# A causal mask added on VectorE in PSUM in place of a matmul with the identity, in a two-layer transformer block

## What is computed

```python
def masked_softmax(s, mask):
    sf = jnp.where(mask, s.astype(jnp.float32), NEG)
    m = jnp.max(sf, axis=-1, keepdims=True)
    e = jnp.where(mask, jnp.exp(sf - m), 0.0)
    p = e / jnp.maximum(jnp.sum(e, axis=-1, keepdims=True), TINY)
    return p.astype(s.dtype)
...
    def blk(args):                                   # latent attention (MLA)
        qb, tq = args
        s = jnp.einsum('bhqd,bhkd->bhqk', qb, k) * scale
        p = masked_softmax(s, tq[:, None] >= pos[None, :])
        return jnp.einsum('bhqk,bhkd->bhqd', p, v)
```

## Time and profile before

| | |
|---|---|
| median of 3 runs | 1611.4 us (1610.57 to 1613.26) |
| the profiled execution: its own time | 1606.89 us |
| the profiled execution: its span | 1605.1 us |
| granted TensorE clock, mean of the core | 0.993 of full speed |
| attention stage of layer 1 | about 152 to 372 us of the span |
| attention stage of layer 2 | about 948 to 1168 us of the span |

### The profile page before, as it was taken

One profiled execution on the slowest core, in us unless ns is written; L12 is line 12 of the kernel. 1 busy time (PEld: TensorE's weight loads), 2 busy tenths in 40 slices (PEclk: granted clock), 3 DMA queues, 4 the chain that ended last, 5 costly groups with the idle time before them and its releaser, 6 DMA issues.

```text
span 1605.1 us, 23249 instructions
## 1 busy us (share of the span) xinstructions
PE 1535.0 (96%) x7566; PEld 1264.9 (79%) x7566; DVE 883.3 (55%) x1342; ACT 722.9 (45%) x1315; POOL 431.5 (27%) x454
## 2 busy tenths in 40 slices
PE   6999999899999999999999999998989999999996
PEld 4888788777788888888888878877867888888885
DVE  5764655665654453535566655556556545444455
ACT  5853666764332222213366546767624322222232
POOL 0301566666111010102011025757750201010010
PEclk9999999999999999999999999999999999999998
DMA  5243221024323232232323412111243222323222
GB/s 186 85 140 125 73 72 66 36 67 145 123 89 103 92 104 92 93 103 92 99 77 128 163 61 65 68 66 41 89 161 105 87 98 92 105 91 100 96 92 105
DMA packets 43526, 155.55 MB, mean 97 GB/s; under 512 B 5312, under 2 KB 5312, under 8 KB 43424
## 3 DMA queue, kind: packets, MB, share of 16 engines
q1 hardware_dynamic: 37440, 134.23, 25.2%
q0 software_dynamic: 5408, 17.95, 3.2%
q10 hardware_dynamic: 576, 2.10, 0.4%
HBM read 143.78 MB, written 10.49 MB: 96 GB/s over the span
## 4 chain that ended last, share of the span: by engine, by line
PE 78%; DVE 8%; issue 6%; ACT 5%; POOL 2%; DMA 1%; DVEq 0%; ACTq 0%; POOLq 0%
PE G L1321 13%; PE G L1323 12%; PE G L1322 12%; PE O L1321 8%; PE O L1322 8%; PE O L1323 8%; PE O L1587 2%; PE T L1563 2%; PE S L1546 2%; POOL wsplit L463 1%; ACT wsplit L562 1%; DVE nmx L1096 1%; PE T L1321 1%; PE T L1322 1%; PE T L1323 1%
## 5 line engine op out<-in xcount | busy, mean ns | idle before, releaser
L562 ACT ACTIVATE wsplit<-stage 128x1024 fp32r<-128x1024 f32 x230 | 243.5, 1059 | 608.7 <-PE G L1323 288.2
L884 DVE TENSOR_TENSOR wsplit<-stage,wsplit 128x1024 fp32r<-128x1024 f32 x190 | 275.6, 1451 | 79.2 <-ACT wsplit L562 79.2
L1321 PE MATMUL G<-xg,wsplit 128*128 128x512 f32 x592 | 244.5, 413 | 15.6 <-DVE xg L888 13.7
L555 POOL TENSOR_TENSOR F<-Y 128x512 f32<-128x512 f32 x64 | 68.4, 1069 | 625.7 <-DVE Y L1291 625.7
L1323 PE MATMUL G<-xg,wsplit 128*128 128x512 f32 x592 | 232.8, 393 | 0.0
L1322 PE MATMUL G<-xg,wsplit 128*128 128x512 f32 x592 | 232.2, 392 | 0.0
L1096 DVE TENSOR_REDUCE nmx<-S 128x1 f32<-128x512 f32 x192 | 93.3, 486 | 106.5 <-PE S L1554 105.1
L719 ACT ACTIVATE F<-S,nmx 128x512 f32<-128x512 f32 x192 | 101.5, 528 | 95.9 <-DVE nmx L1096 95.6
L1321 PEld LDWEIGHTS G<-xg,wsplit 128*128 128x128 f32 x592 | 113.0, 191 | 38.7 <-DVE xg L888 16.2
L1323 PEld LDWEIGHTS G<-xg,wsplit 128*128 128x128 f32 x592 | 111.9, 189 | 24.6
L1321 PE MATMUL G<-area,wsplit 128*128 128x512 f32 x320 | 124.9, 390 | 5.0 <-DVE wsplit L884 5.0
(11 more groups left out here) (249 smaller groups left out, 3086.6 us busy)
## 6 DMA issues: line engine op xcount, KB each, us to landing
stage<-units SPq DMA_DIRECT2D x230, 512.0 KB, 3.3
stage_n<-units_n SPq DMA_DIRECT2D x22, 512.0 KB, 3.5
gates<-Y POOLq DMA_DIRECT2D x32, 256.0 KB, 3.0
E<-gates POOLq DMA_DIRECT2D x16, 256.0 KB, 3.1
F<-gates POOLq DMA_DIRECT2D x16, 256.0 KB, 3.0
x<-x_in ACTq DMA_DIRECT2D x4, 512.0 KB, 11.6
out<-F SPq DMA_DIRECT2D x6, 256.0 KB, 2.1
rope<-tables POOLq DMA_DIRECT2D x1, 768.0 KB, 10.2
```

The costliest lines, as they stand in the source:

```text
L555: pool.tensor_tensor(F[:, m % 2, :], Y[:, m % 2, :], Y[:, m % 2, :], ALU.mult)\
L562: act.activation(wslot(u)[:, 0, :], staged(u), ACT.Copy).then_inc(s_whin if u in SN else s_whi, 1)
L884: dve.tensor_tensor(wslot(u)[:, 1, :], staged(u), wslot(u)[:, 0, :], ALU.subtract)\
L1321: pe.matmul(dst, a(0), b(0), start=first, stop=False)
```

## The change

The identity matmul leaves `scores`, and the last score matmul now closes the group and posts `s_scores`. VectorE, after its wait for `s_scores`, adds the bf16 mask to the last 128 columns of the scores, in place in PSUM, waits for that instruction by a semaphore of its own (`chain`, `s_dvec`), and takes the maximum.

```diff
                 def max_of(i):
                     w = (JOBS[i][3] + 1) * P
                     dve.wait_ge(s_scores, l * NJ + (i + 1))
+                    diagonal = SB[i % 2][:, w - P:w]
+                    chain.mark(dve.tensor_tensor(diagonal, diagonal, causal, ALU.add))
+                    chain.wait()
                     dve.tensor_reduce(nmx[:, i % 4:i % 4 + 1], SB[i % 2][:, 0:w], AX.X, ALU.max, negate=True)\
                         .then_inc(s_max, 1)
...
                     if i < NSA_NJ:
                         for c in range(2):
-                            pe.matmul(dst[:, 0:w], QS[:, 2 * t + e, qt * P:w], KN[:, br, t // 2, c, 0:w],
-                                      start=(c == 0), stop=False)
+                            ins = pe.matmul(dst[:, 0:w], QS[:, 2 * t + e, qt * P:w], KN[:, br, t // 2, c, 0:w],
+                                            start=(c == 0), stop=(c == 1))
                     else:
...
-                        three(dst[:, 0:w], lambda c: MQ[:, t % 2, e, c, qt * P:w], lambda c: MK[:, t % 2, e, c, 0:w],
-                              True, False)
-                    pe.matmul(dst[:, qt * P:w], identb, causal, start=False, stop=True).then_inc(s_scores, 1)
+                        ins = three(dst[:, 0:w], lambda c: MQ[:, t % 2, e, c, qt * P:w],
+                                    lambda c: MK[:, t % 2, e, c, 0:w], True, True)
+                    ins.then_inc(s_scores, 1)
```

## The result

The changed kernel is slower: 1627.3 us median (1626.0 to 1628.1), against 1611.0 us for the kernel before on the same chip; the ratio is 1.0107, with a 95% interval of 1.0086 to 1.0128. I had forecast 1603 us. The two profiled executions have spans of 1626.3 and 1605.1 us.

What follows compares the result with a forecast made beforehand. TensorE was taken to bound most of the attention stages. Terms -24 + 3.5 + 6.4 + 4.2 + 1.6 = -8.3 us gave 1598.6 from the profiled 1606.9, shifted to 1603 us at the median; range 1593 to 1614.

Steps and rivals of the forecast that it cites:

- What bounds the kernel now: Attention stages: TensorE bounds most of the stage, so work removed from it shortens the kernel; another chain ends last in some stretches.
- The mask's time on TensorE: Each of 192 mask matmuls costs TensorE 0.04 + 0.08 us, taken as 0.125 us: 24 us removed.
- Rival 4: TensorE step behind a score group: the 0.08 us stays, only 6.6 us come back; +5.6 us, 1617; chance 0.06.
- Forfeited gain: 3.5 us: At 28 places where TensorE already waits for L1106, removing the mask gains nothing further: 28 x 0.125 us lost.
- The price of a pair: VectorE's add before the maximum: 0.27 us plus 0.03 us dependent wait, 0.30 us each, 58 us of VectorE.
- Rival 3: VectorE between scores and maximum: the add is dear, 0.5 to 0.65 us a pair; +1.7 to +9 us; chance 0.12.
- The slow place of L1076: A small VectorE operation took 0.65 us at one place, 0.18 at another; used as the add's worst price.
- The waits: 6.4 + 4.2 + 1.6 = 12.2 us: New TensorE waits: 28 for L1106 at 0.23 us, 14 score groups at 0.3, 8 value matmuls at 0.2.
- The 104 late maxima: Of 192 VectorE maxima, 104 come late with scores ready; said to carry delays on if the gain is eaten.
- rival 2: Room at TensorE's waits shrinks further, twice as many score groups become tight at 0.5 us: +1.5 us, 1613; chance 0.15.
- the three places: TensorE waits at value matmuls behind L1106, score groups behind ScalarE's exponential, and value matmuls not yet waiting: 6.4, 4.2, 1.6 us.
- my shift by 4.5 us from the profiled execution to the median: The median, 1611.4 us, lay 4.5 us above the profiled 1606.9, so 1598.6 was raised to 1603 us.

Runs made afterwards that it cites:

- the fills: Matmuls of no effect in three of TensorE's waits in each layer; added to the kernel before: 1606.0 us, to the kernel without any mask: 1594.9 us.
- the SBUF add above: Kernel before, mask still on TensorE, plus an unused 128-column SBUF-to-SBUF VectorE add behind L1106 at each step: 1628.6 us.
- the kernel that adds in the clean stretches alone: Kernel before with VectorE adding the mask only in jobs 16 to 32 and 40 to 56 of each layer, plus the fills: 1602.7 us.

## Why the prediction was wrong

- **What bounds the kernel now.** Right for the two clean stretches, 34 of 96 jobs, and wrong for much of the rest. I read from 94% of TensorE in the stages that a microsecond taken from it is nearly a microsecond gained. But full and weak slices are stretches of different kinds, and a weak one isn't a full one with a few waits in it: in jobs 4 to 16, 32 to 40 and 56 to 95 another chain sets the pace of many jobs. With the masks away and the fills in, the jobs outside the clean stretches give back 2.9 us in layer 1 of the 7 that their 64 masks cost.
- **The mask's time on TensorE.** A term mis-sized a little. From the start of a sparse score group to the start of the second matmul behind it, the median falls from 611, 677, 790 and 906 ns to 536, 555, 670 and 780 ns for groups of 128 to 512 columns: 0.075 us at 128 columns, where the step behind the group stays at 0.28 us, and 0.12 to 0.13 at the others, 0.11 in the mean. That is 21 us, not 24. Rival 4 has its part in the 128-column groups alone. By the Trainium skill (VectorE: DVE Perf Modes, the cycle table under the TRN2 errata) a matmul of 128 columns takes 134 cycles, an estimate of 0.056 us at 2.4 GHz; the trace shows twice that behind groups of 256 columns and more.
- **Forfeited gain: 3.5 us.** This is the first step that failed. With the three fills in both kernels, taking the masks away gives 11.1 us (1594.9 against 1606.0 us). So 10 us of the 21 are forfeited, most of it in the jobs outside the clean stretches and not at 28 places.
- **The price of a pair.** Right: 294 ns and 0.32 us from its start to the maximum's, against 0.30. Rival 3 did not happen, and still the kernel is slower. The slow place of L1076 on which I built it looks like the case of the SBUF add above: it ends 0.03 us after GpSimd's L463 (170.27 and 170.24 us). The add in PSUM was never stretched so.
- **The waits: 6.4 + 4.2 + 1.6 = 12.2 us.** The second step that failed, and the larger one. At the same clock the changed kernel is 14 us slower (1620.2 us, the two executions with fills at 0.993, against 1606.2), so with 11 us gained the pairs cost 25 us. I counted a delay once at each place where TensorE waits already or nearly. But a step of VectorE's stream that has no idle time passes on each pair: 12 jobs, from 4 to 16, lose 2.7 us, 0.22 us each, all of the delay that I had worked out for one job. The 104 late maxima were the sign of it: in layer 1 the scores are ready for 9 of the 32 maxima of the clean stretches and for 43 of the other 64. I had them in rival 2, with too low a price: I doubled one term where the whole count was of the wrong kind.
  Of the three places, the waits for L1109 came near the forecast (38 times, 37.4 us, against 28 to 36 times and about 30 us), and those of the score groups did not (1.1 to 3.0 us at the same 2 places, for 4.2).
- **What is queued on the other engines.** Missing from the sum. ScalarE waits for the maximum with its copies and evacuations behind it, and GpSimd for the reciprocals with the MLA weight split behind them. Both came back to TensorE: through the evacuation that waited 1.67 us for ScalarE above, and through GpSimd's weight split, from 4.8 to 9.0 us (L1324 behind L463).
- **The clock.** Missing too. It costs the changed kernel 7 us (1627.3 against 1620.2, of two executions alone) and the kernel before 5 (1611.0 against 1606.2), so it explains only some 2 us of the difference of the medians. It also shows that my shift by 4.5 us from the profiled execution to the median had no ground: a median of the kernel before is not its profile plus an offset, it is an execution with a slower clock.

Balance against the median: -11 (masks) + 25 (pairs) + 2 (clock) = +16 us. The 25 is what is left over, and good to some 2 us: the mean clock also counts the last 12 to 15 us of every profile, which stand at half. A count without mean clocks comes near: the kernel that adds in the clean stretches alone and the one that adds in all others, both with fills, have no fall of the clock in the attention stages, and their traces take -5.5 and +17.9 us over the jobs of both layers, +12.4 together, where the equal clocks above gave 14.

The best kernel found adds the mask on VectorE in jobs 16 to 32 and 40 to 56 only and keeps TensorE busy in three waits: 1602.7 us, 0.4% faster than before. Over the kernel before with the same fills it is 3.3 us. Its trace has 2.75 us gained in each layer's stage, and one more fall of the clock in the second output projection (at 1175 us), which the fill there did not prevent.

What stays open: how much of the 25 us is load and how much is the longer way to the maximum, for which an add that takes the same time behind the maximum would be needed; and why jobs 56 to 60 give 0.5 us back when jobs 40 to 56 were fast.

## What to carry to other kernels

Before work is moved from a busy engine to a less busy one, split the stage into stretches and ask of each which engine's queue has no idle time; utilisation over the whole stage (59% for VectorE here) hid it, and by stretch it showed (50% against 61 to 70%), as did the count of instructions that found their input ready. An instruction ahead of one that several engines wait for can delay every queue behind it. A control load must be timed in its own trace before it is called the same load. And a change can be right for a third of its places: choose the places by the traces of each half alone.

## What the hardware showed that I had not expected

- Taking work from TensorE can cost clock. Without the masks its granted clock stood at half in seven places of the attention stages and output projections that the profile before doesn't have, each time within 2 us behind a gap of 1.6 to 2.7 us from the start of one matmul to the next. Such a gap isn't enough by itself: the profile before has two of 2.3 us with no fall behind them. Nor is it always there: at 880 us that profile has the clock at half for 3.4 us with no gap in front. Matmuls without effect in such waits kept the clock at full in most places: 1600.9 us became 1594.9 with the masks gone, 1627.3 became 1622.3 with the change.
- The same kernel's executions differ with it: 1604.3 us at a mean clock of 0.995 to 1617.1 at 0.986, about 1.4 us for each 0.001. Nothing else was seen to differ between them, but only one was profiled.
- An add of 128 columns on VectorE took 272 to 300 ns in PSUM (192 of 192) and 273 ns to 2.2 us on SBUF alone, and each of the 80 long ones ended 0.14 to 0.16 us after a GpSimd instruction.
- After a score group of 128 fp32r columns the second matmul behind still comes 0.28 us after the first, not 0.23, though no mask stands between; after wider groups it is 0.23.
